# Recurrent layer of an eight-layer network: the fourth input product, its eviction and its convolution go ahead of the first four heads' gates and roots

## The reference, cut to what matters

```python
def recurrent_mixer(h, w_in, conv_w, conv_b, ga_w, ga_b, gx_w, gx_b, lam, w_out):
    y_branch, x_branch = jnp.split(h @ w_in, 2, axis=-1)
    y_branch = jax.nn.gelu(y_branch)
    xc = causal_depthwise_conv(x_branch, conv_w) + conv_b
    xh = xc.reshape(B, S, LRU_HEADS, LRU_HEAD_DIM)
    r = jax.nn.sigmoid(jnp.einsum('bshi,hij->bshj', xh, ga_w).reshape(B, S, LRU_WIDTH) + ga_b)
    i = jax.nn.sigmoid(jnp.einsum('bshi,hij->bshj', xh, gx_w).reshape(B, S, LRU_WIDTH) + gx_b)
    log_a = -LRU_C * r.astype(jnp.float32) * jax.nn.softplus(-lam.astype(jnp.float32))
    a = jnp.exp(log_a)
    mult = jnp.sqrt(jnp.maximum(-jnp.expm1(2.0 * log_a), 0.0))
    mult = jnp.where(jnp.arange(S)[None, :, None] == 0, 1.0, mult)
    b = mult * (i * xc).astype(jnp.float32)
    _, hs = lax.associative_scan(combine, (a, b), axis=1)
    return (y_branch * hs.astype(h.dtype)) @ w_out
```

## Time and profile before

| | us |
|---|---|
| median of 3 runs (lowest, highest) | 2026.59 (2026.11, 2028.11) |
| the profiled execution, its own time | 2026.11 |
| its span, from the first to the last instruction | 2024.3 |
| TensorE busy in the span | 1936.0 (96%) |
| VectorE busy | 1565.8 (77%) |
| ScalarE busy | 1240.5 (61%) |
| mean granted TensorE clock | 0.991 of full |
| recurrent layer, from TensorE's first product of x to the end of its output product | 935.3 to 1018.6 |

### The profile page before, as it was taken

One profiled execution on the slowest core, in us unless ns is written; L12 is line 12 of the kernel. 1 busy time (PEld: TensorE's weight loads), 2 busy tenths in 40 slices (PEclk: granted clock), 3 DMA queues, 4 the chain that ended last, 5 costly groups with the idle time before them and its releaser, 6 DMA issues.

```text
span 2024.3 us, 26201 instructions
## 1 busy us (share of the span) xinstructions
PE 1936.0 (96%) x9320; PEld 1615.6 (80%) x9320; DVE 1565.8 (77%) x1881; ACT 1240.5 (61%) x1461; POOL 162.1 (8%) x228
## 2 busy tenths in 40 slices
PE   8999988899988999999999999999999999999998
PEld 7877877778778788888878778888888888888886
DVE  7765976767667555456878898989889898898987
ACT  6551146645655534345777767777777777777775
POOL 5013402323011000000000000000000000000000
PEclk9999999999999999999999999999999999999999
DMA  8422234325324355553569999899999989999994
GB/s 342 151 79 105 104 114 144 122 104 188 115 94 167 113 200 187 187 187 104 203 236 383 353 355 377 343 380 352 371 375 350 374 344 384 352 371 374 344 374 172
DMA packets 71802, 504.78 MB, mean 249 GB/s; under 512 B 8864, under 2 KB 8864, under 8 KB 11808
## 3 DMA queue, kind: packets, MB, share of 16 engines
q1 hardware_dynamic: 70432, 498.87, 65.2%
q0 software_dynamic: 1280, 4.72, 0.6%
HBM read 501.46 MB, written 2.10 MB: 249 GB/s over the span
## 4 chain that ended last, share of the span: by engine, by line
PE 84%; DVE 8%; ACT 5%; issue 2%; POOL 1%; DMA 0%; DVEq 0%; SPq 0%; ACTq 0%; POOLq 0%
PE psum L1022 24%; PE psum L1024 24%; PE psum L1023 24%; PE psum L1958 4%; DVE low L989 3%; ACT high L986 2%; PE psum L3486 1%; PE psum L1966 1%; ACT h L1694 1%; PE psum L3417 0%; PE psum L1974 0%; DVE small L1738 0%; PE psum L1566 0%; PE psum L1143 0%; PE psum L1590 0%
## 5 line engine op out<-in xcount | busy, mean ns | idle before, releaser
L989 DVE TENSOR_TENSOR low<-raw,high 128x2048 fp32r<-128x2048 f32 x459 | 1044.7, 2280 | 264.6 <-ACT high L986 261.1
L986 ACT ACTIVATE high<-raw 128x2048 fp32r<-128x2048 f32 x459 | 877.0, 1912 | 371.3 <-PE psum L1024 351.6
L1022 PE MATMUL psum<-high,yT_high 128*128 128x512 f32 (+1 forms) x1672 | 664.0, 397 | 25.7 <-DVE yT_low L3693 6.5
L1024 PE MATMUL psum<-high,yT_low 128*128 128x512 f32 (+1 forms) x1672 | 653.2, 391 | 0.0
L1023 PE MATMUL psum<-low,yT_high 128*128 128x512 f32 (+1 forms) x1672 | 651.9, 390 | 0.0
L1022 PEld LDWEIGHTS psum<-high,yT_high 128*128 128x128 f32 x1672 | 315.2, 189 | 95.3 <-issue 14.3
L1024 PEld LDWEIGHTS psum<-high,yT_low 128*128 128x128 f32 x1672 | 315.1, 188 | 66.9
L1023 PEld LDWEIGHTS psum<-low,yT_high 128*128 128x128 f32 x1672 | 315.7, 189 | 61.0
L1022 PE MATMUL psum<-high,hT_high 128*128 128x512 f32 (+2 forms) x560 | 219.8, 393 | 1.7 <-DVE low L1006 0.9
L1024 PE MATMUL psum<-high,hT_low 128*128 128x512 f32 (+2 forms) x560 | 216.7, 387 | 0.0
L1023 PE MATMUL psum<-low,hT_high 128*128 128x512 f32 (+2 forms) x560 | 216.6, 387 | 0.0
(11 more groups left out here) (367 smaller groups left out, 1715.6 us busy)
## 6 DMA issues: line engine op xcount, KB each, us to landing
raw<-in_moe_weights SPq DMA_DIRECT2D x336, 1024.0 KB, 4.9
raw<-in_weights SPq DMA_DIRECT2D x132, 1024.0 KB, 4.9
raw<-in_weights SPq DMA_DIRECT2D x2, 896.0 KB, 4.6
raw<-in_weights SPq DMA_DIRECT2D x2, 768.0 KB, 8.2
x<-in_x SPq DMA_DIRECT2D x2, 512.0 KB, 4.1
raw<-in_weights SPq DMA_DIRECT2D x2, 512.0 KB, 3.6
rows<-h POOLq DMA_DIRECT2D x1, 1024.0 KB, 5.0
out_x<-x SPq DMA_DIRECT2D x1, 1024.0 KB, 5.7
```

What stands on the lines that cost most here:

```text
L986: eng.activation(high, raw, ACT.Copy).then_inc(k.high_ready, 1)
L989: eng.tensor_tensor(low, raw, high.bitcast(F32), ALU.subtract).then_inc(k.low_ready, 1)
L1022: pe.matmul(out, lhs.high, rhs.high, start=start, stop=False)
L1024: return pe.matmul(out, lhs.low, rhs.high, start=False, stop=stop)
```

## The change

x 3 stands directly behind x 2 on every engine. TensorE computes x 0 to x 3, then the gates of heads 0 to 3, then y 0. ACT evicts x 3 ahead of those gates instead of between the decays and the roots. DVE convolves the fourth pair ahead of `root_inputs(range(4))` instead of behind it. Nothing is added or removed; the gates' weights are loaded one place later, behind x 3's, and the rest of SP's list keeps its order.

```diff
 def r_order():
 
     first, last = [("gates", h) for h in range(4)], [("gates", h) for h in range(4, R_HEADS)]
-    return [("x", 0), ("x", 1), ("x", 2)] + first + [("x", 3), ("y", 0)] + last + [("y", 1), ("y", 2), ("y", 3)]
+    return [("x", 0), ("x", 1), ("x", 2), ("x", 3)] + first + [("y", 0)] + last + [("y", 1), ("y", 2), ("y", 3)]
@@ r_scalar
-    for i in range(3):
+    for i in range(4):
         x(i)
     gates(range(4))
     act.wait_ge(k.r_decay_ready, 1)
     decays(range(4))
-    x(3)
     roots(range(4))
     ahead(k, act, ("r", "y", 0))
     gates(range(4, R_HEADS))
@@ r_vector
     conv(1)
     conv(2)
-    v.wait_ge(k.r_conv_ready, 6)
-    root_inputs(range(4))
     conv(3)
     v.wait_ge(k.r_conv_ready, KC)
+    root_inputs(range(4))
     ahead(k, v, ("r", "y", 0))
     scans(range(4))
```

## The result

The changed kernel takes 2032.03 us in the median of 20 runs (2026.90 to 2034.73), the kernel before 2027.62 in 20 runs beside it (2025.70 to 2030.87). The ratio is 1.0018, with a 95% interval of 1.0012 to 1.0025: slower, by a little less than the 0.2% that I had called measurable. I had predicted 2028.4 in a range of 2026.2 to 2031.0, so the measured median lies outside.

What follows compares the result with a forecast made beforehand. The layer's end was bound by ACT until the first decays, then DVE; ACT's 5.79 us delay less 0.60, 1.96 and 1.4 left +1.8 on 2026.11, giving 2027.9, or 2028.4 as a median, range 2026.2 to 2031.0.

Steps and rivals of the forecast that it cites:

- ACT's idle time ahead of x 3: ACT between the split of y 1 and x 3's eviction: nothing to do for 3.4 us, with four heads' gates waiting behind.
- its delay at the three table loads: ACT's table loads for first gates, second gates and gelu: 5.79, 3.2 and 1.9 us late.
- its new wait for the gelu: DVE at `gated(0)`: waits 1.9 us for ACT's first gelu, ready at 991.4 instead of before DVE asks.
- the late end of DVE: DVE's last low part ends 1.8 us late, so the second half of the output product starts at 1007.1.
- the step on the clock: TensorE's first output half: a clock fall of 3.4 us at half rate loses 1.7 us, which is covered.
- one such fall costs nothing: After one short clock fall the first output half ends at 1007.0, just under 1007.1; forecast with this case, chance 0.70.
- A long fall: Clock rival in the first output half: 6.9 us at half rate lose 3.4, making the sum +3.4, 2029.5; chance 0.14.
- the late gelu: ACT's first gelu ends at 991.3 instead of 989.43, putting DVE and the layer's end 1.8 us behind.
- The removed waits: TensorE's waits before x 3 (1.28) and head 6's gates (1.34) go, but return as one of 4.1 before the output product.
- late gelu does not happen: Rival: ACT makes up more than counted, leaving only DVE's 0.3 us gain: -0.3 us, 2025.8; chance 0.08.
- removed waits count in full: Rival: all three TensorE waits in the stretch are won, 3.94 us less, 2022.2; chance 0.02.
- ACT makes nothing up: Rival: ACT's second gates stay 5.79 us late like the first; sum +4.3, 2030.4, 0.21% slower; chance 0.06.

Runs made afterwards that it cites:

- the late split: Changed kernel with ACT's split of y 2 behind the first roots instead of ahead of the first gates; x 2's eviction to expert layer's first small transpose took 71.48 us.
- the early low part: Kernel before with the low part of y 1 formed ahead of the first root inputs, in DVE's wait for the decays; ratios 1.0002 and 0.9997.

## Why the prediction was right or wrong

**The direction and the mechanism: right.** Each named piece came out. ACT's idle time ahead of x 3 (3.4 us, measured 3.36), its delay at the three table loads (5.8, 3.2 and 1.9 us, measured 5.75, 3.25, 1.95), DVE's wait for the decays (3.7; 3.77), its new wait for the gelu (1.9; 1.90), TensorE without a wait from x 3 to y 3 and then one of 4.1 (4.28), the late end of DVE (1.8; 1.83). The experiments with Copy for Sqrt in both kernels show that ACT's work behind x 3 carries the loss; the late split shows that its order does not.

**The size: wrong, in the step on the clock.** I wrote that "one such fall costs nothing", took its length of 3.4 us from 935 to 940, where only short pauses precede it, and gave this case 0.70. A long fall had 0.14 and was priced at +3.4. What came behind the wait of 4.3 us was the long fall, of 6.8 to 6.9 us, in all three profiles of the changed kernel and in that with the late split; the short one came only with Copy, behind a wait of 2.6. My price for the long fall was too high as well. I took all of it to fall on work, but 1.1 us of it passed in the wait, and a slow matmul takes 0.43 us, less than twice 0.2275. The thirteen slow matmuls cost 2.5 us; the late gelu covers 1.8 of it, and 0.7 show. The term of the clock is +0.7 (0.9 in the later two profiles), not 0 and not 1.6, and the sum +2.5 to +2.7, not +1.8. By the Trainium skill (TensorE: Matmul & The Clock Gate, HAM oscillation — how this bites in real kernels) the burst behind a long wait starts cold; the trace agrees, in each of the four profiles. That much the prediction had taken from it; the length of the fall it had to set itself, and set too short.

**The base and the set: too low.** The three runs of before that I had gave 2026.59; twenty gave 2027.62. I had the scatter of 2 us before me and put it in the range, but centred the range on the low value. That is 1.0 of the 3.6 us between 2028.4 and 2032.03, and the clock in the layer is 0.7. The remaining 1.9 are no part of the sum and do not lie in the layer. Of the 20 runs of the set 13 are in the slower of the two groups above, so the median is one of that group, whose runs take some 4 us more. The same program gave +0.18%, +0.06% and +0.21% in three sets. That the first median fell outside the range is thus in part the luck of the set; that the sum was 0.7 to 0.9 short is not.

**The removed waits.** That their 2.6 us would not be won was right, and so was the place where they come back. The rivals "late gelu does not happen", "removed waits count in full" and "ACT makes nothing up" are all excluded by ACT's rows.

**What I missed.** I had counted the new wait of TensorE as neutral, since the two that go give almost its length, and had priced the clock behind it by a fall that followed shorter pauses. A rearrangement that turns two waits of 1.3 us into one of 4.3 is not neutral for TensorE even if the total is.

**What stays open** is why the execution of before in the profile ran its first 954 us 5.7 us faster than the first one of the changed kernel. Profiles of both kernels and of all variants fall into 953.5 to 955.9 and 959.8 to 960.2 for the first mark; each of the four latter has a clock fall at 634 or 651 us that none of the others has. Counted from the clock recorded in the traces, these four are at the half level for 37.5 us before the first mark, the eight others for 27.3. The 10.2 us more account for up to 5.1 us of time, so the difference is in the main one of the clock, and it occurs in kernels with and without the change. What decides which of them comes was not tried.

## What to carry to other kernels

Before moving a product ahead of work that another engine waits for, measure that engine's margin at the next hand-over (0.24 us here), and count how long it will stand idle behind the moved product (3.4 us) less what it finds already done later on (the eviction, the split, its own waits). Waits of TensorE are not additive: one long wait in place of several short ones can bring the clock down, and the slow matmuls behind it belong in the sum. When the change is 2 us in 2000, compare a stretch between two marks in the profiles, which repeats to 0.2 us, and not the medians, which need dozens of runs and jump by some 4 us when more than half of a set falls into the other group.

## What the runs showed of the hardware that I had not expected

What the clock does behind a wait is not fixed by the wait alone. The same wait of 2.21 us near 1165 us left the clock at 1.00 in the kernel before and brought it to a mean of 0.64 over 4 us in the first profile with the early low part, and a fall there in both profiles took back a gain of 1.4 us. A wait of 4.3 us in the layer was followed by 6.9 us at the half level, one of 2.6 us by 3.4, and around one of 8.6 it lasted 10.2; with 30 matmuls in it of which nobody reads the result there was no fall. In one set of the unchanged kernel, the runs of a mean clock of 0.988 took 2030.2 us and those of 0.991 took 2026.2 (13 and 12 runs), 4 us apart with not one instruction different.
